# Layer changes reordered, and the third layer's value projection by input chunks of 1024 columns, in a four-layer float32 transformer stack on one core

## The reference

```python
hn = rmsnorm(x, odd_norm[i])
q, k, v = jnp.split(hn @ odd_w_in[i], 3, axis=-1)
...
x = x + mixed
hn = rmsnorm(x, ffn_norm[layer])
x = x + (jax.nn.silu(hn @ ffn_w_gate[layer]) * (hn @ ffn_w_up[layer])) @ ffn_w_down[layer]
```

## Time and profile before

| | us |
|---|---|
| median of three runs | 1588.44 |
| lowest, highest | 1585.86, 1589.16 |
| span of the profiled execution | 1589.6 |

### The profile page before, as it was taken

How to read it: one execution, slowest core, us unless ns; L and a number is a source line. 1 busy time by engine, 2 the same in 40 slices (tenths; PEclk the granted TensorE clock), 3 DMA queues, 4 the chain that set the end, 5 groups by cost and what they waited for, 6 DMA issues and landing times.

```text
span 1589.6 us, 30962 instructions
## 1 busy us (share of the span) xinstructions
PE 1542.5 (97%) x10555; PEld 1359.0 (85%) x10555; DVE 1193.6 (75%) x2322; ACT 863.2 (54%) x1323; POOL 263.7 (17%) x110
## 2 busy tenths in 40 slices
PE   7899999999999999999999999999999999999998
PEld 6777888899878887898899999988888888878887
DVE  7987888725788887666599853499999999975555
ACT  7765444568754445755556566455555444444553
POOL 2001000165100001100468856500000000000000
PEclk9999999999999999999999999999999999999999
DMA  6134565533465555423445555555554555555554
GB/s 226 54 101 162 188 191 192 185 133 120 146 200 187 187 194 172 146 93 107 172 160 173 172 186 183 187 171 172 172 172 161 176 173 177 172 172 195 190 196 146
DMA packets 72557, 264.67 MB, mean 167 GB/s; under 512 B 8080, under 2 KB 8336, under 8 KB 72112
## 3 DMA queue, kind: packets, MB, share of 16 engines
q1 hardware_dynamic: 71744, 261.00, 49.7%
q10 hardware_dynamic: 752, 2.83, 0.5%
HBM read 262.75 MB, written 1.05 MB: 166 GB/s over the span
## 4 chain that ended last, share of the span: by engine, by line
PE 86%; DVE 3%; ACT 2%; issue 1%; DMA 0%; ACTq 0%; DVEq 0%; SPq 0%
PE ps L550 17%; PE ps L639 11%; PE ps L640 10%; PE ps L651 10%; PE ps L554 9%; PE ps L538 7%; PE ps L542 6%; PE ps L539 6%; PE ps L1085 2%; PE ps L584 1%; PE ps L586 1%; PE ps L592 1%; DVE arena L1687 1%; DVE w_lo L1687 1%; ACT w_hi L1176 1%
## 5 line engine op out<-in xcount | busy, mean ns | idle before, releaser
L1176 ACT ACTIVATE w_hi<-ring 128x1024 fp32r<-128x1024 f32 x489 | 515.8, 1057 | 338.0 <-PE ps L651 206.7
L1687 DVE TENSOR_TENSOR w_lo<-ring,w_hi 128x1024 fp32r<-128x1024 f32 x388 | 473.1, 1220 | 95.3 <-ACT w_hi L1176 81.1
L2544 POOL TENSOR_TENSOR w_lo<-ring,w_hi 128x1024 fp32r<-128x1024 f32 x101 | 255.1, 2537 | 751.3 <-DVE w_lo L1687 379.6
L550 PE MATMUL ps<-hT,w_hi 128*128 128x512 f32 x1216 | 308.9, 395 | 3.5 <-DVE hT L1725 2.6
L639 PE MATMUL ps<-w_hi,halves_hi 128*128 128x512 f32 x688 | 271.5, 395 | 2.5 <-DVE w_lo L1687 1.9
L640 PE MATMUL ps<-w_hi,halves_lo 128*128 128x512 f32 x688 | 268.7, 391 | 0.0
L550 PEld LDWEIGHTS ps<-hT,w_hi 128*128 128x128 f32 x1216 | 220.8, 189 | 47.7 <-issue 3.0
L538 PE MATMUL ps<-hT,w_hi 128*128 128x256 f32 x984 | 247.7, 289 | 6.1 <-DVE hT L1725 4.0
L539 PE MATMUL ps<-hT,w_hi 128*128 128x256 f32 x984 | 243.2, 284 | 0.0
L538 PEld LDWEIGHTS ps<-hT,w_hi 128*128 128x128 f32 x984 | 189.8, 193 | 11.3 <-issue 7.7
L539 PEld LDWEIGHTS ps<-hT,w_hi 128*128 128x128 f32 x984 | 190.1, 193 | 0.0
(11 more groups left out here) (301 smaller groups left out, 1587.9 us busy)
## 6 DMA issues: line engine op xcount, KB each, us to landing
ring<-in_strips SPq DMA_DIRECT2D x489, 512.0 KB, 3.4
const<-in_const SPq DMA_DIRECT2D x1, 1352.0 KB, 11.5
x_s<-in_x SPq DMA_DIRECT2D x2, 512.0 KB, 4.3
arena<-in_rel ACTq DMA_DIRECT2D x1, 1024.0 KB, 5.7
arena<-in_keys ACTq DMA_DIRECT2D x1, 1024.0 KB, 6.7
out<-x_s SPq DMA_DIRECT2D x4, 256.0 KB, 2.3
arena<-in_ssm_bc SPq DMA_DIRECT2D x1, 512.0 KB, 6.6
arena<-in_ssm_b SPq DMA_DIRECT2D x1, 512.0 KB, 7.8
```

The lines of the kernel that those rows point to most:

```text
L550: pe.matmul(bank, w[0][:, c * P:(c + 1) * P], hT[:, c].rearrange("p s t -> p (s t)"), start=c == 0, stop=False, skip_group_check=True)
L1176: sc.activation(w_hi[:, n % RING, :], ring[:, n % RING, :], ACT.Copy).then_inc(high_ready, 1)
L1687: return ve.tensor_tensor(o, a, b, op)
L2544: po.tensor_tensor(w_lo[:, n % RING, :], ring[:, n % RING, :], w_hi[:, n % RING, :].bitcast(F32), ALU.subtract).then_inc(low_ready, 1)
```

## The change

The last strip of each MLP gets its low half from GpSimd instead of VectorE. The raw transposes of the first token block move between and behind the last strip's groups, into other banks. The first gate and up strips of an MLP are multiplied as a pair: all products with high inputs first, chunk by chunk, in operations of 256 columns, then those with low inputs. The strips of the value projection hold one input chunk by all 1024 columns; each is multiplied in twelve operations of 512 columns into four banks that are copied out behind the eighth strip. `turned`, `hT_high` and `hT_low` count chunks instead of pairs of chunks. The diff, cut:

```diff
+SCALE_BANK = {1: 2, 2: 5, 3: 2}
+VALUE_BANKS = (4, 6, 2, 3)
+NORM_BANKS = [(0, 1, 2, 3)] + [(5, 7, 0, 1)] * 4 + [(7, 4, 0, 1)]
...
             def input_ready(fresh, c):
-                if fresh is not None and c % 2 == 0:
-                    pe.wait_ge(hT_low, 4 * fresh + c // 2 + 1)
+                if fresh is not None:
+                    pe.wait_ge(hT_low, KC * fresh + c + 1)
+
+            def high_input_ready(fresh, c):
+                if fresh is not None:
+                    pe.wait_ge(hT_high, KC * fresh + c + 1)
...
+            def strip_pair(banks, ws, fresh):
+                first, second = banks
+                for c in range(KC):
+                    cols = slice(c * P, (c + 1) * P)
+                    high_input_ready(fresh, c)
+                    pe.matmul(first[:, 0:T], ws[0][0][:, cols], hT_hi[:, c, :], start=c == 0, stop=False,
+                              skip_group_check=True)
+                    if c == 0:
+                        low_halves(ws[0])
+                    pe.matmul(first[:, 0:T], ws[0][1][:, cols], hT_hi[:, c, :], start=False,
+                              stop=c == KC - 1, skip_group_check=True)
+                    pe.matmul(second[:, 0:T], ws[1][0][:, cols], hT_hi[:, c, :], start=c == 0, stop=False,
+                              skip_group_check=True)
+                low_halves(ws[1])
+                for c in range(KC):
+                    pe.matmul(second[:, 0:T], ws[1][1][:, c * P:(c + 1) * P], hT_hi[:, c, :], start=False,
+                              stop=c == KC - 1, skip_group_check=True)
+                for bank, w in zip(banks, ws):
+                    for c in range(KC):
+                        input_ready(fresh, c)
+                        mm = pe.matmul(bank[:, T:2 * T], w[0][:, c * P:(c + 1) * P], hT_lo[:, c, :],
+                                       start=False, stop=c == KC - 1, skip_group_check=True)
+                    mm.then_inc(strip_done, 1)
...
+            def values(j):
+                w = split(AT[("odd", "v", j)])
+                def times(a, b, x, part, stop=False):
+                    return pe.matmul(ps[:, VALUE_BANKS[2 * a + b], :], x[:, j, a * P:(a + 1) * P],
+                                     w[part][:, 512 * b:512 * b + 512], start=j == 0 and x is hT_hi and part == 0,
+                                     stop=stop)
+                if j == KC - 1:
+                    input_ready(2, j)
+                    low_halves(w)
+                    for a in range(NT):
+                        for b in range(2):
+                            times(a, b, hT_hi, 0)
+                            times(a, b, hT_lo, 0)
+                            mm = times(a, b, hT_hi, 1, True)
+                        if a == 0:
+                            mm.then_inc(v_half, 1)
+                else:
+                    high_input_ready(2, j)
+                    for part in range(2):
+                        if part:
+                            low_halves(w)
+                        for a in range(NT):
+                            for b in range(2):
+                                times(a, b, hT_hi, part)
+                    input_ready(2, j)
+                    for a in range(NT):
+                        for b in range(2):
+                            mm = times(a, b, hT_lo, 0)
+                mm.then_inc(strip_done, 1)
...
+            def turn_x(i, a, b):
+                pe.wait_ge(x_ready, 4 * (i - 1) + 2 * a + b + 1)
+                for c in range(4 * b, 4 * b + 4):
+                    mm = pe.transpose(norm_at(i, c)[:, a * P:(a + 1) * P], x_s[:, a, c * P:(c + 1) * P], ident)
+                    if a == NT - 1:
+                        mm.then_inc(turned, 1)
...
                 if i in SCALED_OUT:
-                    raw_norm(i)
+                    for b in range(2):
+                        turn_x(i, NT - 1, b)
...
-            def rows(w, hi, lo, first, last):
+            def rows(w, hi, lo, first, last, turn=None):
...
+                        if turn in SCALED_OUT and a and not b:
+                            turn_x(turn, 0, 0)
...
                 mm.then_inc(strip_done, 1)
+                if turn in SCALED_OUT:
+                    turn_x(turn, 0, 1)
...
-                gate_up(base, 4, fresh=STAGE_OF[name])
+                strip_pair((ps[:, 4, :], ps[:, 6, :]), (split(base), split(base + 1)), STAGE_OF[name])
                 widen_scale(STAGE_OF[name])
...
             def odd():
-                for g in range(4):
-                    proj_tm_pair(("odd", "v"), g, None if g else 2)
-                    if g == 0:
+                for j in range(KC):
+                    values(j)
+                    if j == 2:
                         widen_scale(2)
...
+                    if j == 0:
+                        pe.wait_ge(evac, values_out - 3)
+                        strip_fm(ps[:, 4, 0:T], split(AT[("odd", "q", 0)]))
...
+                high_to(AT[("odd", "v", 7)] + RING - 1)
+                sc.wait_ge(diag_ready, 2 * NT + NT)
+                for a in range(NT):
+                    if a == 0:
+                        sc.wait_ge(v_half, 1)
+                    else:
+                        sc.wait_ge(strip_done, AT[("odd", "v", 7)] + 1)
+                    for b in range(2):
+                        sc.activation(o_v[:, a, 512 * b:512 * b + 512], ps[:, VALUE_BANKS[2 * a + b], :], ACT.Copy,
+                                      scale=stat[:, 4 + a:5 + a]).then_inc(evac, 1)
...
                 combine(at + 1, FC - 1)
-                low(at + 3)
...
-            po.wait_ge(low_ready, AT[("odd", "v", 0)])
-            lows(("odd", "v", 0), ("odd", "v", 7))
+            po.wait_ge(low_ready, AT[("mlp0", "down", FC - 1)])
+            lows(("mlp0", "down", FC - 1), ("odd", "v", 7))
...
-            po.wait_ge(low_ready, AT[("mix", "if", 0)])
-            lows(("mix", "if", 0), ("mix", "qa", 1))
+            po.wait_ge(low_ready, AT[("mlp1", "down", FC - 1)])
+            lows(("mlp1", "down", FC - 1), ("mix", "qa", 1))
```

## The result

The changed kernel takes 1595.39 us (median of 4 runs, 1594.24 to 1595.99), the kernel before 1587.83 (4 runs, 1585.86 to 1589.16): **slower**, ratio 1.0048, 95% interval 1.0036 to 1.0060, +7.6 us. The prediction said 1595.9, range 1582 to 1600, with 0.59 on slower. The profiled execution took 1595.23 us; its span, from first to last instruction, is 1593.4.

A forecast was written before the change was run, and what follows sets the result against it. The prediction took TensorE, busy 97% of the span, as the bound. Its terms, -3.6 + 4.4 + 4.4 + 4.7 - 1.9 - 0.5, gave +7.5 us on a median of 1588.44: 1595.9 us, range 1582 to 1600.

The forecast's parts named there:

- Part 1: First MLP's entry: running two strips as a pair ends them earlier and moves everything behind, -3.6 us.
- Part 2: Both MLP ends: GpSimd's low halves and VectorE's relay take turns, so TensorE starts the last strip later, +4.4 us each.
- Part 3: Behind both MLP ends: TensorE's clock falls after idling 5.5 us, +2.6 us at the first, +2.1 at the second.
- Part 4: Value strips: 25.66 us becomes 23.7 despite a new 0.9 us wait in the third strip, -1.9 us.
- Part 5: Moved transposes 0; second MLP's entry 0, as ScalarE is held by issuing loads; waiting per chunk -0.5 us.
- finer counts: Entries of mix and peer: waiting per chunk instead of per two saves two 256-column matmuls each, -0.5 us together.
- Rivals A to C: MLP ends: only first GpSimd operation obstructs, 1582.8 us (0.14); no obstruction, 1580.2 (0.11); one turn lost each, 1587.0 (0.07).
- A: MLP ends: only the first GpSimd operation obstructs VectorE, +0.2 us each, no clock lost; 1582.8 us, chance 0.14.
- Rival D: First MLP's entry: the strip pair brings nothing because its waits and separate signals slow it; 1599.5 us, chance 0.06.

The follow-up runs named there:

- e2: Changed kernel, but GpSimd, after cutting the last down strip's low half, waits for VectorE's relay to finish before cutting the next strips; 1584.20 us.
- e1: Changed kernel with only the last down strip's low half moved back from GpSimd to VectorE at both MLP ends; 1581.49 us.
- e3: Kernel before, with only the last down strip's low half moved from VectorE to GpSimd at both MLP ends; 1598.01 us.
- e5: e1 with the strip pair also undone: each MLP entry runs its two wide strips one after the other, by input chunk; 1586.03 us.
- e6: e1 with the third layer's value strips also undone: four pairs of strips, weights held, 256-column matmuls; 1582.02 us.
- e4: Changed kernel plus 20 useless 512-column matmuls on TensorE ahead of the last down strip at both MLP ends; 1589.41 us.
- e10: e1 run once more, unedited; 1584.02 us.
- e9: e1 with the last down strips' low-weight products last, plus 8 useless matmuls ahead of the normalisation at the second MLP's end; 1581.03 us.

## Why the prediction was right

Differences after minus before, from the two traces:

| step | predicted | measured |
|---|---|---|
| Part 1, first MLP's entry | -3.6 | -3.5 |
| Part 2, first end | +4.4 | +4.3 |
| Part 3, clock, first end | +2.6 | +2.6 |
| Part 4, value strips | -1.9 | -1.8 |
| Part 5, second MLP's entry | 0 | -1.4 |
| Part 2, second end | +4.4 | +4.3 |
| Part 3, clock, second end | +2.1 | +1.35 |
| Part 5, finer counts | -0.5 | -0.5 |
| sum | +7.5 | +5.4; +6.0 at the last matmul |

- **Part 2** is the verdict, and its working held: the order of the turns, 5.28 us of wait for 5.5, VectorE's subtraction as releaser. The Trainium skill (SBUF — State Buffer, Who interferes with whom) says that the first to issue has the ports shared by VectorE and GpSimd for the whole instruction; the turns above agree, each VectorE operation ending 0.15 to 0.28 us after a low half does. The Trainium skill states this for VectorE's two-port modes; the add and the multiply, with two inputs in SBUF, did the same here. Rivals A to C fell on this. e2 shows that A was a real case, for a kernel whose GpSimd has only one low half queued: 0.26 us more wait than in e1.
- **Part 1**: the broadcast was expected at 129.8 and came at 130.03. But 1.4 of the 3.5 us hang on a clock fall that the kernel before had in its profile and that e3, with the same entry, had not. The prediction put that share at about 1 us and took the fall as part of the kernel; of the three profiles with the old entry (before, e3, e5) one has it. Rival D is out: e5 loses 1.8 and 1.1 us without the pair.
- **Part 3**: right at the first end, 0.75 too high at the second. The term mixed the rows of two other stages, and for one of them, the start, the profile's clock reads 1.00 (7.0 to 11.3 us), so no row showed that its 2.0 us were the clock's. The prediction let the whole fall meet work; here it began in the idle time, where it costs nothing, and e3 shows 1.7 and 1.0 for the same two stalls. That 2.6 came out exactly is partly luck.
- **Part 4**: the new wait in the third strip is 0.61 us, expected 0.9. Its -1.8 is from the traces, and e6's trace gives 1.6; the time of e6 could not confirm it.
- **Part 5, second entry, failed.** I took the 1.90 us issue of the earlier trace rows for the price of that load and let ScalarE be the bound either way, so the term was 0; it measured -1.4. The 1.90 isn't the price of the load. The DMA view of the kernel before, 444 to 447.5 us (queue, kind: packets, MB, share), has an instruction load in that stretch, the kernel after none, nor any of the others but e3, and in before and e3 alone the issue takes 1.8 to 1.9:

```profile
q10 hardware_dynamic: 93, 0.76, 70.9%
q8 instruction: 1, 0.02, 2.4%
```

  With the issue at 0.45, ScalarE's next high half starts at 447.07 (446.88 before) although its work ahead of it began 1.6 us later, and the pair's gain comes through; without the pair and with the short issue the entry is 1.1 us longer (e5). In the kernel before the load's packet runs from 445.06 for 1.35 us, inside the issue (444.88 to 446.78), and in e3 from 451.00 for 1.20 us, inside 450.73 to 452.56. That the instruction load is what stretched the issue is argued from their standing together, not shown by a run.
- **Finer counts**: as predicted, 0.24 at each entry. At the peer's, the transposing matmuls come 5.69 us later than before (777.69 against 772.00), the first strip's products with the low half of the weights only 5.45 (784.72 against 779.27). At the mix ScalarE's norm parts come 5.85 later (638.55 against 632.70), its copies of the strips behind 5.60. e1, which keeps the finer counts, has both steps; e3, which lacks them, has neither.

The terms make 5.4, and the strips at 781 us stand 5.45 later than before. Another 0.6 us comes between 1033 and 1205 us, in the peer layer, where e3's and before's strips keep their distance; no run here explains it. The medians are 7.6 us apart, the two spans only 3.8: the profiled execution of the kernel before has 2.2 us more behind its last matmul, and the fall of 1.4 at 127. Without these two the spans would be 7.4 apart, an estimate that fits the medians but that no run shows.

So the verdict rests on a mechanism that was shown, and the number partly on misses that cancel: the second entry (-1.4 missed) and the second clock term (0.75 too high) made the forecast too high, the priced fall at 127 (if most executions lack it) and the 0.6 us in the peer layer too low. With clock falls of 1.4 to 3.0 us that come and go, agreement to 0.5 us is closer than the method can promise.

## What to carry to other kernels

Before work goes to an engine that looks idle, ask what runs beside it: each of the three 2.4 us GpSimd operations that ran beside the chain of short VectorE operations on SBUF cost VectorE 1.4 to 2.0 us, so the price grows with the number queued. If it must go there, let it wait for the end of the chain (e2), or give it work of which no more than one piece is ready. Price a stall of TensorE with the clock behind it, and when two kernels differ by less than such a fall, compare their traces landmark by landmark.

## What the runs showed of the hardware

- VectorE and GpSimd took turns at the MLP ends, where both had SBUF work queued: an add, a multiply and a cast of 0.3 to 0.45 us each took 1.87, 2.46 and 2.31 us, GpSimd's own low halves 2.41 to 2.52. An operation reading PSUM took its usual 0.69 beside them.
- Around each wait of 5.28 us of TensorE (the changed kernel, e3) the granted clock was at 1.2 GHz for 3.4 to 6.9 us; with 4.70 us of useless matmuls in that time it stayed at 2.4 GHz (e4).
- The clock also fell with TensorE busy throughout, and differently in two executions of one kernel (e1, e10).
- An issue of a DMA by ScalarE took 0.45 or 1.9 us for the same load, the longer one where an instruction load fell beside it (argued from before and e3 against the ten others).
- The lowest medians are e9's (1581.03) and e1's (1581.49). e1 is the whole change without the step to GpSimd, 6.4 us below the kernel before, or 4.0 in its repetition (1584.02); e2 and e6 to e9 lie in or near that spread and aren't ranked by these runs.
